# The up projection's high x high and high x low products issued as one 512-column product

## The reference

```python
D_MODEL, SEQ, DEPTH, D_FF, CONV_WIDTH = 1024, 256, 2, 2816, 3

def conv_ffn(h, w_up, conv_w, conv_b, w_down):
    u = h @ w_up                      # (256, 1024) @ (1024, 5632)
    c = lax.conv_general_dilated(
        u, conv_w[:, None, :], window_strides=(1,), padding=((CONV_WIDTH - 1, 0),),
        dimension_numbers=('NWC', 'WIO', 'NWC'), feature_group_count=u.shape[-1]) + conv_b
    gate, val = jnp.split(c, 2, axis=-1)
    return (jax.nn.silu(gate) * val) @ w_down

for l in range(DEPTH):
    ...                               # the mixers
    h = rms_norm(x, norm_ffn[l])
    x = x + conv_ffn(h, ffn_w_up[l], ffn_conv_w[l], ffn_conv_b[l], ffn_w_down[l])
```

## Time and profile before

| | |
|---|---|
| median of three timed runs | 995.14 us |
| the profiled execution | 994.98 us |
| its span | 993.3 us |
| TensorE busy | 950.7 us (96%) |
| VectorE busy | 743.3 us (75%) |
| ScalarE busy | 565.7 us (57%) |
| GpSimd busy | 340.1 us (34%) |
| granted TensorE clock | 0.999 of full speed |
| one step of the MLP's loop | 16.98 us |

### The profile page before, as it was taken

One profiled execution on the slowest core, in us unless ns is written; L12 is line 12 of the kernel. 1 busy time (PEld: TensorE's weight loads), 2 busy tenths in 40 slices (PEclk: granted clock), 3 DMA queues, 4 the chain that ended last, 5 costly groups with the idle time before them and its releaser, 6 DMA issues.

```text
span 993.3 us, 17232 instructions
## 1 busy us (share of the span) xinstructions
PE 950.7 (96%) x6447; PEld 817.6 (82%) x6447; DVE 743.3 (75%) x1240; ACT 565.7 (57%) x905; POOL 340.1 (34%) x267
## 2 busy tenths in 40 slices
PE   6899899998999999999999999999999999999997
PEld 5789666776878999999989976777777799999996
DVE  5989999985666767677865679998747676666666
ACT  6435665757454555555564466766764555555544
POOL 0111666672330573156400046667516001111010
PEclk9999999999999999999999999999999999999999
DMA  8963433335454755555469433234545445555551
GB/s 226 235 216 92 132 118 128 123 90 170 137 169 158 202 180 201 170 193 186 131 165 262 146 109 126 87 129 123 155 139 170 135 140 200 193 187 173 199 178 43
DMA packets 135864, 156.83 MB, mean 158 GB/s; under 512 B 16400, under 2 KB 103032, under 8 KB 135800
## 3 DMA queue, kind: packets, MB, share of 16 engines
q1 hardware_dynamic: 135800, 155.98, 50.3%
HBM read 154.92 MB, written 1.05 MB: 157 GB/s over the span
## 4 chain that ended last, share of the span: by engine, by line
PE 71%; DVE 16%; ACT 6%; issue 3%; POOL 2%; DMA 1%; SPq 0%; DVEq 0%; ACTq 0%; POOLq 0%; PEldq 0%
PE pj L734 51%; PE bX L734 6%; PE bA L734 5%; DVE wl L1554 5%; PE bB L734 4%; PE bY L1083 2%; DVE s5x L1883 1%; ACT wh L1260 1%; DVE work L1847 1%; PE bY L734 1%; DVE bnat L1883 1%; POOL s5h L2142 1%; PE bX L1072 1%; DVE gate L1570 1%; DVE hl L1576 1%
## 5 line engine op out<-in xcount | busy, mean ns | idle before, releaser
L1554 DVE TENSOR_TENSOR wl<-ring,wh 128x1024 fp32r<-128x1024 f32 (+1 forms) x276 | 364.6, 1324 | 134.8 <-ACT wh L1260 133.3
L1260 ACT ACTIVATE wh<-ring 128x1024 fp32r<-128x1024 f32 (+1 forms) x276 | 288.9, 1048 | 243.3 <-PE pj L734 200.6
L734 PE MATMUL pj<-hh,wh 128*128 128x256 f32 x1024 | 293.2, 286 | 6.2 <-DVE wl L1554 4.3
L734 PE MATMUL pj<-hl,wh 128*128 128x256 f32 x1024 | 289.7, 283 | 0.0
L734 PE MATMUL pj<-hh,wl 128*128 128x256 f32 x1024 | 289.6, 283 | 0.0
L734 PEld LDWEIGHTS pj<-hh,wh 128*128 128x128 f32 x1024 | 196.2, 192 | 11.2 <-issue 5.6
L734 PEld LDWEIGHTS pj<-hl,wh 128*128 128x128 f32 x1024 | 196.3, 192 | 1.2 <-issue 0.5
L734 PEld LDWEIGHTS pj<-hh,wl 128*128 128x128 f32 x1024 | 196.3, 192 | 0.0
L734 PE MATMUL pj<-wh,hl 128*128 128x512 f32 (+1 forms) x416 | 168.6, 405 | 6.6 <-DVE wl L1554 1.9
L734 PE MATMUL pj<-wh,hh 128*128 128x512 f32 (+1 forms) x416 | 159.7, 384 | 0.0
L734 PE MATMUL pj<-wl,hh 128*128 128x512 f32 (+1 forms) x416 | 159.4, 383 | 0.0
(11 more groups left out here) (315 smaller groups left out, 1471.3 us busy)
## 6 DMA issues: line engine op xcount, KB each, us to landing
ring<-in_ffn_w_up SPq DMA_DIRECT2D x44, 1024.0 KB, 5.1
ring<-in_w_in SPq DMA_DIRECT2D x40, 1024.0 KB, 5.1
ring<-in_ffn_w_down SPq DMA_DIRECT2D x22, 1024.0 KB, 5.0
ring<-in_w_in SPq DMA_DIRECT2D x16, 512.0 KB, 5.2
ring<-in_w_branch SPq DMA_DIRECT2D x8, 1024.0 KB, 5.1
ring<-in_w_out SPq DMA_DIRECT2D x8, 1024.0 KB, 5.1
ring<-in_w_branch SPq DMA_DIRECT2D x8, 512.0 KB, 6.1
ring<-in_w_in SPq DMA_DIRECT2D x8, 256.0 KB, 5.1
```

Source lines behind the costliest of these rows:

```text
L734: return nc.tensor.matmul(o, a, b, start=start, stop=stop, skip_group_check=True)
L1260: A(dst, src, ACT.Copy).then_inc(w_hi.sem, 1)
L1554: TT(dst, src, hi.bitcast(F32), ALU.subtract).then_inc(w_lo.sem, 1)
```

## The change

`hh` and `hl` become the two halves of one tensor `h2`, so that one product can stream 512 columns: 256 of the high part, then 256 of the low. In `up`, each row block k now has two products in place of three: `wh` by both halves into all 512 columns of a bank, and `wl` by the high half, added to the first 256 columns. Each piece now has a bank of its own, so a unit takes two: `pjs[i]` is a pair of banks, whose second is the former `bO` or `bY`.

The result is the sum of a bank's two halves. ScalarE copies the low halves of both banks to SBUF (`lows`, into `ups`, which lies in the tensor `kr`, free in this phase), VectorE adds the first halves to it (`whole`), and this add frees the banks. `conv` and `taps` then read `ups` in SBUF. `conv` waits for `whole`; Silu and the product wait for a new semaphore, `cv_done`, of the taps. The idle products at a layer's end go to `bO` and wait for `unit_out` too. `split_hi` and `split_lo` move within a step so that `lows` and `whole` stand early.

```diff
-        hh = sb("hh", [P, KD, T], F32R)
-        hl = sb("hl", [P, KD, T], F32R)
+        h2 = sb("h2", [P, 2, KD, T], F32R)
+        hh, hl = h2[:, 0], h2[:, 1]
...
+        ups = [kr[:, 2 * i:2 * i + 2, :] for i in range(2)]
...
-        pj = [bank(f"pj{i}") for i in range(2)]
+        pjs = [ctx.enter_context(nc.psum_tensor(f"pj{i}", [P, 2, 512], F32)) for i in range(2)]
+        pj = [pjs[i][:, 0, :] for i in range(2)]
         bX = [bank(f"bX{i}") for i in range(2)]
-        bY = bank("bY")
+        bY = pjs[1][:, 1, :]
...
-        bO = bank("bO")
+        bO = pjs[0][:, 1, :]
...
                     for m in range(2):
-                        piece(l, s + m, pj[n % 2][:, T * m:T * m + T], turn * TURN)\
-                            .then_inc(w_used.sem, 1)
+                        pe.wait_ge(w_lo.sem, w_lo.at(l, s + m + 1) + turn * TURN)
+                        hi, lo = (w[:, (s + m) % SPLIT, :].rearrange("p (k n) -> p k n", k=KD) for w in (wh, wl))
+                        o = pjs[n % 2][:, m, :].rearrange("p (c t) -> p c t", c=2)
+                        for k in range(KD):
+                            if s + m == S_FFN and k % JC == 0:
+                                pe.wait_ge(h_ready.sem, h_ready.at(l, 11 + k // JC))
+                            mm(o, hi[:, k, :], h2[:, :, k, :], k == 0, False)
+                            ins = mm(o[:, 0, :], lo[:, k, :], hh[:, k, :], False, k == KD - 1)
+                        ins.then_inc(w_used.sem, 1)
...
                 pe.wait_ge(w_lo.sem, w_lo.at(l, s + 1))
-                idle(6)
+                n = U_FFN + 2 * STEPS - 2
+                pe.wait_ge(unit_out[0].sem, unit_out[0].at(l, n // 2 + 1))
+                idle(6, bO)
...
-                def conv(n, e, tile, turn=0, times=1):
+                def lows(n, turn=0, times=1):
 
                     t, k = summed(n)
                     a.wait_ge(t.sem, t.at(l, k) + turn * TURN)
+                    A(ups[n % 2], pjs[n % 2][:, :, T:2 * T], ACT.Copy).then_inc(lows_out.sem, 1)
+                    lows_out.made += times
+
+                def conv(n, e, tile, turn=0, times=1):
+
+                    a.wait_ge(unit_out[n % 2].sem, unit_out[n % 2].at(l, n // 2 + 1) + turn * 2)
                     for m in range(2):
-                        ins = A(cv[:, e, T * m:T * m + T], pj[n % 2][:, T * m:T * m + T], ACT.Identity,
+                        ins = A(cv[:, e, T * m:T * m + T], ups[n % 2][:, m, :], ACT.Identity,
...
+                def whole(n, turn=0, times=1):
+
+                    v.wait_ge(lows_out.sem, lows_out.at(l, n - U_FFN + 1) + turn * 4)
+                    TT(ups[n % 2], pjs[n % 2][:, :, 0:T], ups[n % 2], ALU.add).then_inc(unit_out[n % 2].sem, 1)
+                    unit_out[n % 2].made += times
+
                 def taps(n, e, tile, turn=0, times=1):
 
-                    u = unit_out[n % 2]
                     v.wait_ge(cv_last.sem, cv_last.at(l, n - U_FFN + 1) + turn * 4)
...
-                            ins = STT(dst, pj[n % 2][:, T * m:T * m + T - back],
+                            ins = STT(dst, ups[n % 2][:, m, 0:T - back],
...
-                            ins.then_inc(u.sem, 1)
+                            ins.then_inc(cv_done.sem, 1)
...
                     split_lo(l, s + 3, turn, times)
-                    if cc:
-                        split_lo(l, s + 4, turn, times)
+                    whole(U_FFN + 2 * cc, turn, times)
+                    split_lo(l, s + 4, turn, times)
                     taps(U_FFN + 2 * cc, 0, c * 2, turn, times)
-                    if cc:
-                        split_lo(l, s + 5, turn, times)
-                    if cc < STEPS - 1:
-                        split_lo(l, s + (6 if cc else 4), turn, times)
-                    if not cc:
-                        split_lo(l, s + 5)
+                    split_lo(l, s + 5, turn, times)
+                    whole(U_FFN + 2 * cc + 1, turn, times)
+                    if 0 < cc < STEPS - 1:
+                        split_lo(l, s + 6, turn, times)
                     taps(U_FFN + 2 * cc + 1, 1, c * 2 + FT, turn, times)
```

More of the change, by code:

```diff
@@ L455, in build @@
         cv_mid = sem("cv_mid", 2 * STEPS)
+        cv_done = sem("cv_done", 2 * STEPS)
+        lows_out = sem("lows_out", 2 * STEPS)
         sg_ready = sem("sg_ready", STEPS)
@@ L748, in piece @@
                 for k in range(KD):
-                    if s == S_FFN and k % JC == 0:
-                        pe.wait_ge(h_ready.sem, h_ready.at(l, 11 + k // JC))
                     mm(o, hi[:, k, :], hh[:, k, :], k == 0, False)
@@ L804, in turn_merged, with idle @@
                 turn(mr, t, h)
-            def idle(n):
+            def idle(n, o=bY):
                 for _ in range(n):
-                    mm(bY[:, 0:P], ident, ident, True, True)
+                    mm(o[:, 0:P], ident, ident, True, True)
             pe.wait_ge(ident_in.sem, 16)
@@ L1487, in ffn_step @@
                     split_hi(l, s + 3, turn, times)
+                    lows(U_FFN + 2 * cc, turn, times)
+                    split_hi(l, s + 4, turn, times)
                     if cc:
-                        split_hi(l, s + 4, turn, times)
                         a.wait_ge(a_ready.sem, a_ready.at(l, cc) + turn * 2)
                     conv(U_FFN + 2 * cc, 0, c * 2, turn, times)
-                    if cc:
-                        split_hi(l, s + 5, turn, times)
-                    if cc < STEPS - 1:
-                        split_hi(l, s + (6 if cc else 4), turn, times)
-                    if not cc:
-                        split_hi(l, s + 5)
+                    split_hi(l, s + 5, turn, times)
+                    lows(U_FFN + 2 * cc + 1, turn, times)
+                    if 0 < cc < STEPS - 1:
+                        split_hi(l, s + 6, turn, times)
                     conv(U_FFN + 2 * cc + 1, 1, c * 2 + FT, turn, times)
-                    n = U_FFN + 2 * cc
-                    a.wait_ge(unit_out[n % 2].sem, unit_out[n % 2].at(l, n // 2 + 1) + turn * 2)
+                    a.wait_ge(cv_done.sem, cv_done.at(l, 2 * cc + 1) + turn * 4)
                     A(cv[:, 0, :], cv[:, 0, :], ACT.Silu).then_inc(sg_ready.sem, 1)
@@ L2001, in taps @@
                         else:
-                            ins.then_inc(u.sem, 1)
+                            ins.then_inc(cv_done.sem, 1)
                     cv_mid.made += times
-                    u.made += times
+                    cv_done.made += times
                 def ffn_step(c, cc, turn=0, times=1):
@@ L2022, in ffn_step @@
                         v.wait_ge(sg_ready.sem, sg_ready.at(l, cc + 1))
-                        v.wait_ge(unit_out[n % 2].sem, unit_out[n % 2].at(l, n // 2 + 1))
+                        v.wait_ge(cv_done.sem, cv_done.at(l, 2 * cc + 2))
                         TT(aT[:, cc % 2, :], cv[:, 0, :], cv[:, 1, :], ALU.mult).then_inc(a_ready.sem, a_ready.up())
@@ L2177, in product @@
                     g.wait_ge(sg_ready.sem, sg_ready.at(l, cc + 1) + turn * 2)
-                    g.wait_ge(unit_out[n % 2].sem, unit_out[n % 2].at(l, n // 2 + 1) + turn * 2)
+                    g.wait_ge(cv_done.sem, cv_done.at(l, 2 * cc + 2) + turn * 4)
                     g.wait_ge(a_split.sem, a_split.at(l, cc - 1) + turn * 2)
```

4 lines of the change are left out of this document (1 added, 3 removed).

## The result

The changed kernel takes 1000.07 us (median of 5 runs, 999.98 to 1000.42); before 995.14 (994.49 to 995.96). The ratio is 1.0051, with a 95% interval of 1.0039 to 1.0062. I had forecast 992.2 and a range that ended at 998.0: it is slower by 4.9 us where I expected 2.9 faster.

What follows compares the result with a forecast made beforehand. TensorE, busy for 96% of the span, was taken as the bound. Terms -9.4 + 2.6 + 0.5 + 3.2 = -3.1 us, with 0.2 given back for slower taps: -2.9, so 992.2 us, range 987.5 to 998.

Steps and rivals of the forecast that it cites:

- stream, 704 pairs: TensorE's up projection: two products replace three per row block, 13.3 ns saved each of 704 times, 9.4 us less.
- wait ahead of piece 6, both layers: Step 0 to step 1: added copy and add delay piece 6's split; TensorE waits 1.3 us, twice, 2.6 us.
- second layer's end: Copy and add delay the lower split ahead of the idle products; the last products start later, costing 0.5 us.
- first layer's waits and end: First layer's last steps: taps queue with GpSimd's table products, so TensorE waits; 3.2 us in sum.
- 0.120 + 0.227 = 0.347: Up projection: a narrow plus a wide product in turn take 0.347 us, border gain and loss cancelling.
- Both bounds: Pair of wide and narrow products in turn: 0.340 us at least, 0.356 at most, from rows at two borders.
- rival A: Up projection: each wide product takes 0.236, the pair 0.356; time +2.8 us, 997.9; chance 0.16.
- The fixed part per product: TensorE: each product with its own weight load costs about 13 ns beyond its columns at 2.4 GHz.
- The waits: TensorE's added waits before piece 6 and at both layers' ends: 2.6, 0.5 and 3.2 us.
- The queueing with GpSimd: First layer's last steps: taps with two SBUF inputs wait for GpSimd's table products, up to 0.83 us each.
- rival C: First layer's end: GpSimd doesn't hold up the taps, cost 0.7 not 3.2 us; time 989.7; chance 0.13.

Runs made afterwards that it cites:

- The control of order: Kernel before the change with early small Silu, earlier split of the last but one weight piece, and split of piece 7 ahead of `ah`: 995.04 us, ratio 0.9998.
- the run with the sum in PSUM: Changed kernel with the sum of the halves written back to the PSUM banks, where convolution and taps read it: 995.48 us, ratio 1.000.
- two and two: Changed kernel with products in the order two wide, two narrow in place of strict turn: 998.97 us, one run.
- early Silu: Changed kernel with one small Silu (one column) on ScalarE ahead of step 0 of each layer's MLP: 1000.06 us.

## Why the prediction was wrong

By its own steps, against the profiled execution:

| step | forecast, us | measured, us |
|---|---|---|
| stream, 704 pairs | -9.4 (0.347 a pair) | -5.2 (640 at 0.353, 64 at 0.347) |
| down products behind it | 0 | +0.6 (5.50 for 5.47 a step) |
| wait ahead of piece 6, both layers | +2.6 | +3.2 |
| second layer's end | +0.5 | +0.7 |
| first layer's waits and end | +3.2 | +5.4, 1.2 of it the clock |
| sum | -3.1 | +4.7 |

The measured column is from start-to-start times; the MLPs' own lengths give +4.6. The spans differ by 5.1, and the other 0.5 us lie outside the MLPs. Of these, 0.3 are there before the first MLP begins: TensorE's clock was at 1.2 GHz from 112.44 to 115.86 us in this execution, not in the one of before, and the stretch around it took 0.7 us longer. The control of order, whose products are those of before, has the same fall there.

**The step that failed** is "0.120 + 0.227 = 0.347", one border's gain beside the other's loss. The pair in turn took 0.353 in 640 of 704 cases and 0.347 only in the other 64. That is 4.8 of the 7.8 us of the miss, with the slower down products behind it. Both bounds had been read from rows (0.340 and 0.356), and 0.352 was named as the point from which the change costs time: this was rival A, with a chance of 0.16 against 0.38 for the forecast, and the loop's pair came out near it. Taking the middle of two border rows was the error, since neither shows what happens when there is a border at every product. Grouping the products gave the 0.348 that I had forecast. That strict turn reached 0.347 in the second layer's first pieces doesn't save the step: the rate that holds in the loop is the other, and the runs don't show why.

**The fixed part per product** (of a product with its own weight load) was right in itself: in groups a step's 32 blocks take 11.15 us in place of 11.51, 11 ns a block. By the 2.5 ns that the Trainium skill gives (TensorE: Matmul & The Clock Gate, "Wait — 56ns, not 53.3ns?") two products of 768 columns together would take 0.325, an estimate; no order here reached that.

**The waits** had the right places and releasers but were sized too low, 6.3 us in the sum for 9.3 measured, which is the other 3.0 of the miss. One by one: 1.2 to 1.4 us forecast ahead of piece 6, 1.53 and 1.64 measured; 0.9 and 2.6 in the first layer's last step, 1.37 and 2.62; 0.8 at the second layer's end, 0.96. One thing was read too low: the convolution from SBUF takes 0.595, not the 0.50 of an activation of that size, nor the 0.555 from PSUM. The activation of the 0.50 has a scale from a tensor and no bias, the convolution has both. And of GpSimd's product in the earlier trace rows 0.85 us were left when VectorE's split began, not 0.7, so the two durations overlap a little. The queueing with GpSimd was right (rival C falls), and its two sides show in one stretch of the run with the sum in PSUM.

**Not foreseen** was the fall of the clock while TensorE waits at the first layer's end: 1.2 us on the idle products. With it gone the change would still have been slower, by 3.7 us.

**What the sum hid.** A forecast of -3.1 was the difference of 9.4 and 6.3. A tenth off on each side would already be half of it, so the range should have reached past 1000.

## What to carry to other kernels

A fixed cost per product can be saved by merging products, but what the merged stream takes has to be read from that very order: here 704 products fewer gained 5.2 us in strict turn and 7.9 in groups. When an engine of the chain behind gets one more step, look for each wait where the old order had just enough room (here 0.07 us), and expect the next one behind it once the first is mended. An elementwise step on VectorE that is moved from PSUM to SBUF loses its freedom from GpSimd; a sum written back to PSUM kept it and cost nothing in the loop.

## What the runs showed of the hardware

- Products of 512 and 256 columns took 0.353 us a pair in strict turn everywhere behind a layer's first down product, 0.347 or 0.353 ahead of it, and 0.348 in twos or eights. Neither one contiguous read nor other output columns change the 0.353 of the loop.
- Four `scalar_tensor_tensor` (two of 255 columns, two of 254) took 1.8 us with one SBUF input, beside GpSimd's 128x512 products too, and up to 4.55 with two SBUF inputs beside them (1.90 without them).
- ScalarE's Identity with scale and bias at 128x256 took 0.595 us from SBUF and 0.555 from PSUM.
- The granted clock fell to 1.2 GHz for 3.41 us during TensorE's wait of 2.46 us at the first layer's end in the changed kernel's profiled execution. Six profiled executions have this wait, of 2.46 to 2.48 us; the clock fell in three of them (the changed kernel, two and two, early Silu) and not in the other three.
